# A four-layer transformer with a hybrid and an expert layer on one core: the first four mixers' projections and outputs as three rounded products

## The chip, the cores and the metric

The kernel runs on one core of one Trainium2 chip. The metric is the device time of one execution in microseconds (us), as the median over runs. A lower time is better.

## The reference

The input has 256 tokens (SEQ) and a width of 1024 (D). Four layers come first, each a feed-forward block, a mixer and a feed-forward block; a hybrid block and a mixture of experts follow and are no part of the change. What matters here:

```python
for i in range(DEPTH):                      # 4 layers
    x = x + 0.5 * rms_norm(swiglu(rms_norm(x, g[0]), ffn_w_in[i, 0], ffn_w_out[i, 0]), g[1])
    hm = rms_norm(x, g[2])
    if kind == 0:                           # layers 0 and 3: mixer A
        m = sliding_sink_attention(hm, a_w_in[j], a_w_out[j], a_sinks[j], rel_bias)
    elif kind == 1:                         # layer 1: mixer B
        m = nsa_attention(hm, b_w_in[j], b_w_out[j], ...)
    else:                                   # layer 2: mixer C
        m = moba_attention(hm, c_w_in[j], c_w_out[j], rel_bias)
    x = x + rms_norm(m, g[3])
    x = x + 0.5 * rms_norm(swiglu(rms_norm(x, g[4]), ffn_w_in[i, 1], ffn_w_out[i, 1]), g[5])
```

Every mixer is `h @ w_in` (queries of 16 heads of 64, keys, values; in B also six key and value sets and a gate), masked softmax attention with a relative bias, and `o @ w_out`. All inputs and the result are float32.

## The kernel before

Blocks run one after the other: ffn, A, ffn, ffn, B, ffn, ffn, C, ffn, ffn, A, ffn, then the hybrid and the experts. The residual x stays on chip. All weights come from HBM over SyncE's queue (`stream_weights`, L666) into a ring of three slots (`raw_ring`, RING is 3), one load of up to 512 columns or 512 rows in a slot; a slot is loaded again when its readers are done.

The feed-forward blocks (`pe_ffn`, L1289) don't use float32 products. A weight w is split: ScalarE copies it to the rounded type fp32r (w_hi, L1124 and L1131), VectorE subtracts that from the raw weight (w_lo, L1136 and L1143). h is split likewise. A product is then w_hi·h_hi + w_lo·h_hi + w_hi·h_lo, accumulated in PSUM. Lines L1298 and L1350 to L1352 are 512 columns wide (L1298 takes both halves of h beside each other), L1302 is 256.

The mixers use float32 products, which the hardware profile records as two matmuls each:

- `product` (L1411) computes an item: eight products over the eight 128-row parts of D. Form T (L1423) holds 128 columns of weights and moves h transposed (256 tokens): queries and keys. Form N (L1426) holds 128 tokens of h and moves up to 512 weight columns: values (128 wide in A, 256 in B, 512 in C), and B's gate of 48.
- `output` (L1497, product at L1499) multiplies the heads' result oT by the output weights, 512 columns at a time, in two halves c of four 128-row parts. The first half is `output_first`, four groups set between attention steps from `wo_step` on; the second is the mixer's last work on TensorE.

`mixer_layout` writes the order down by hand: the list of items, how many of them run ahead of the attention (`ahead`), and which run in step j (`steps`). A unit is one group of four heads and one half of 128 queries; step j does these on the engines:

- TensorE (L1404): scores of unit j (L1444), transposes of unit j−2 (L1463), the step's items, one `output_first`, values of unit j−2 (L1486 or L1491).
- VectorE (`dve_mixer`, L1555): the softmax coefficients of unit j−1 (L1616 to L1625), scale, bias and maximum of unit j (L1593 to L1608), copies of finished T items out of PSUM times the rows' scale (L1576, L1580), and the heads' result of unit j−2 copied to oT (L1635; added in B, L1633).
- ScalarE (`act_mixer`, L1657): the transposed probabilities of unit j−2 (L1692), the exponentials of unit j with their sums (L1677, in A also the sink, L1680), and N items out of PSUM (L1669).
- POOL (L1709): the probabilities times the coefficients (L1715).

Each engine runs its list in order, so an instruction that waits holds all that stands behind it. In the exponentials' loop VectorE's L1608 of unit j releases ScalarE's L1677, whose last one releases VectorE's L1616, behind which the scale and bias of unit j+1 stand. Item results lie in PSUM banks 2 and 3 in turn, scores in banks 0 and 1, transposes in 4 and 5, head results in 6 and 7.

Before a mixer's items, VectorE finishes the residual update (`dve_update`) and ScalarE makes h from the transposed x (L1014). Where a feed-forward block comes next, `dve_into_folded` (L984) sets the low halves of h (L978) between the parts of that update.

Of the kernel before, what the change touches and what calls it, by code (L numbers as in the profile page):

```python
# [149 lines left out]
class Attn:  # L150
# [11 lines left out]
    def vcol(self, quad, r, s):  # L162
        return {"A": quad // 2, "B": quad + 4 * s, "C": 4 * quad + r, "H": quad}[self.kind] * HD


class Semaphores:


    def __init__(self, nc, ctx):
        def some(names):  # L170
# [32 lines left out]
            some("proj evac_act evac_dve")  # L203

# [41 lines left out]
class Program:  # L246
# [19 lines left out]
    def map_memory(self):  # L266
# [23 lines left out]
        self.hT = new("hT", [P, KT, SEQ])  # L290
        self.gain_at = self.top
# [36 lines left out]
        b_start = self.cur  # L328
        self.zc = mix("cmp_tokens", [P, 2, G_B, SEQ])
# [130 lines left out]
    def plan(self):  # L460
        ins = self.ins
        fill = tile = item = unit = sunit = outs = 0
        split = used = folded = turned = mixers = posts = 0
        ev = {"act": 0, "dve": 0}
        self.fills = []
        for n, b in enumerate(self.blocks):
# [7 lines left out]
            if kind in ("ffn", "moe"):  # L474
                b["f"] = folded
                folded += 1
# [10 lines left out]
            else:  # L487
# [40 lines left out]
    def mixer_layout(self, b):  # L528
# [16 lines left out]
        def Q(f, r):  # L545
            T(f, 128 * (r % 4), self.qT[:, r, :])

        if kind == "A":
# [5 lines left out]
            N(kv, 128, 128, [self.v[:, a, 0:128] for a in range(NT)])  # L554
            for r in range(1, 8):
                Q(qs[r // 4], r)
            b["ahead"] = 6
            b["steps"] = [[6], [7], [8], [9], [10]]
            b["need_qk"] = [4, 6, 8, 10]
            b["need_v"] = [[2, 3]] * 4  # L560
            b["wo_step"] = 6
            wo = ins["a_w_out"][b["j"]]
        elif kind == "B":
# [20 lines left out]
            b["need_qk"] = [7, 9, 11, 13, 14, 14, 15, 15]  # L584
            b["need_v"] = [[4, 5]] * 4 + [[16, 17]] * 4
# [6 lines left out]
        elif kind == "C":  # L592
            w = ins["c_w_in"][0]
            vs, qs, ks = [], [], []
            vs.append(cols(w, (2 * D, 512)))
# [3 lines left out]
            vs.append(cols(w, (2 * D + 512, 512)))  # L599
# [4 lines left out]
            def V(c, a):  # L604
                items.append(dict(form="N", fill=vs[c], a=a, c0=0, n=512, dst=self.v[:, a, 512 * c:512 * c + 512]))

            Q(qs[0], 0), K(0), V(0, 0), V(0, 1), Q(qs[0], 1), K(1), Q(qs[0], 2)
            K(2), Q(qs[0], 3), K(3), Q(qs[1], 4), K(4), Q(qs[1], 5), K(5), V(1, 0)
            Q(qs[1], 6), K(6), Q(qs[1], 7), K(7), V(1, 1)
            b["ahead"] = 7  # L610
            b["steps"] = [[7, 8], [9, 10], [11, 12], [13, 14], [15, 16], [17, 18], [19]]
            b["need_qk"] = [5, 9, 13, 18]
            b["need_v"] = [[2, 3]] * 2 + [[14, 19]] * 2
            b["wo_step"] = 7
# [189 lines left out]

def x_order(b):
# [35 lines left out]
PRE_SS, PRE_V, PRE_R, POST_SS, POST_V, POST_R = 16, 20, 24, 32, 36, 40  # L841
# [133 lines left out]
def dve_low_h(K, dve, b, k):  # L975
# [3 lines left out]
    K.nc.vector.scalar_tensor_tensor(out=K.hT_lo[:, k, :], in0=turned_k(K, k), scalar=g,  # L979
                                     in1=K.hT_hi[:, k, :].bitcast(F32), op0=ALU.mult, op1=ALU.subtract)\  # L980
# [3 lines left out]
def dve_into_folded(K, dve, prev, b):  # L984
# [19 lines left out]
    dve_lo_dn(K, dve, 0, b["fill0"] % RING, b["tile0"] + 1)  # L1004


def act_into_turned(K, act, prev, b):
# [3 lines left out]
    def high(k):  # L1011
        g = K.gcol[:, f * KT + k:f * KT + k + 1]
        act.wait_ge(K.sem.x_tr, KT * f + k + 1)
        K.nc.scalar.activation(K.hT_hi[:, k, :] if folds(b) else K.hT[:, k, :], turned_k(K, k), ACT.Copy, scale=g)\  # L1014
            .then_inc(K.sem.hk_hi, 1)
# [13 lines left out]
    else:  # L1029
# [11 lines left out]
        high(7)  # L1041
    act.wait_ge(K.sem.r2_ps, f + 1)
# [104 lines left out]
def act_ffn(K, act, b):  # L1147
# [2042 lines left out]
```

## Time and profile before

| | before |
|---|---|
| median of 3 runs | 2689.94 us (2687.75, 2689.94, 2694.95) |
| profiled execution, span | 2692.0 us |
| TensorE matmuls, busy | 2642.6 us |
| TensorE weight loads, busy | 2087.1 us |
| VectorE | 1687.4 us |
| ScalarE | 1239.5 us |
| POOL | 239.1 us |
| mean granted TensorE clock | 0.988 |

The page reports one execution. A busy time counts each instruction from start to end; matmuls overlap their successors, so a rate is read from the starts of two groups in the timeline. "x16" is a number of instructions, and a float32 product is two of them. The granted clock is 1.00 at 2.4 GHz and 0.50 at 1.2 GHz.

### The profile page before, as it was taken

To read this page: it belongs to the slowest core of one execution; us is meant where nothing else is said; L and a number is where in the kernel's file an instruction comes from. 1 tells how busy PE (TensorE), PEld (TensorE's weight loads), DVE (VectorE), ACT (ScalarE), POOL (GpSimd) and SP (SyncE) were. 2 spreads that over 40 slices of the span, in tenths; PEclk is the share of its full clock that TensorE was granted. 3 is DMA by queue.
4 is the path that set the end of the run, shared out by engine and by line. 5 is a ranking of instruction groups with operands and counts; after the bars stand their busy time and mean duration, and the time that the engine had idled before them with its cause. 6 is when DMAs were issued, how large, how long until landed. Compare 5 with 4: busy or idle time off the path is not lost.

```text
span 2692.0 us, 36916 instructions
## 1 busy us (share of the span) xinstructions
PE 2642.6 (98%) x13112; PEld 2087.1 (78%) x13112; DVE 1687.4 (63%) x2560; ACT 1239.5 (46%) x1986; POOL 239.1 (9%) x364
## 2 busy tenths in 40 slices
PE   9999999999998999999999999999999999899999
PEld 7887688888874788888768888885888654688887
DVE  6764577777353777775237777745776552577776
ACT  5444544544333545544235455434543222366565
POOL 0001100100111100001010010012000001000000
PEclk9999999999997999999999999999999999999999
DMA  9542455554331555453255546433553322478885
GB/s 322 195 151 88 179 187 187 184 198 159 104 125 62 216 195 191 157 192 136 94 203 196 187 150 221 166 133 144 193 198 114 112 91 73 156 279 287 310 289 196
DMA packets 337244, 472.33 MB, mean 175 GB/s; under 512 B 15632, under 2 KB 275056, under 8 KB 337152
## 3 DMA queue, kind: packets, MB, share of 16 engines
q1 hardware_dynamic: 334464, 464.02, 48.1%
q0 software_dynamic: 2192, 6.94, 0.8%
q8 instruction: 54, 0.88, 0.1%
q14 instruction: 38, 0.31, 0.0%
q10 hardware_dynamic: 496, 0.17, 0.0%
HBM read 470.01 MB, written 1.10 MB: 175 GB/s over the span
## 4 chain that ended last, share of the span: by engine, by line
PE 92%; DVE 4%; ACT 2%; issue 1%; DMA 1%; POOL 0%; SPq 0%; DVEq 0%; ACTq 0%; POOLq 0%
PE psum_all L1298 22%; PE psum_all L1302 12%; PE psum_all L1423 6%; PE psum_all L1350 6%; PE psum_all L1351 6%; PE psum_all L1352 6%; PE psum_all L1499 4%; PE psum_all L1959 4%; PE psum_all L2919 3%; PE psum_all L2900 3%; PE psum_all L2896 3%; PE psum_all L2897 3%; PE psum_all L1426 2%; PE psum_all L2924 1%; PE psum_all L1444 1%; PE psum_all L1463 1%
## 5 line engine op out<-in xcount | busy, mean ns | idle before, releaser
L1298 PE MATMUL psum_all<-hT_both,gu_hi 128*128 128x512 f32 x2688 | 670.9, 391 | 0.3 <-DVE gu_lo L1136 0.3
L1298 PEld LDWEIGHTS psum_all<-hT_both,gu_hi 128*128 128x128 f32 x2688 | 492.8, 188 | 95.4 <-DVE gu_lo L1136 0.6
L1136 DVE TENSOR_TENSOR gu_lo<-raw_ring,gu_hi 128x2048 fp32r<-128x2048 f32 x176 | 402.0, 2286 | 14.1 <-ACT gu_hi L1124 9.6
L1302 PEld LDWEIGHTS psum_all<-hT_both,gu_lo 128*128 128x128 f32 x2688 | 366.7, 190 | 26.2
L1302 PE MATMUL psum_all<-hT_both,gu_lo 128*128 128x256 f32 x2688 | 374.8, 282 | 0.0
L1124 ACT ACTIVATE gu_hi<-raw_ring 128x2048 fp32r (+1 forms) x175 | 334.2, 1912 | 16.1 <-DVE oT L1635 12.2
L1131 ACT ACTIVATE down_hi<-raw_ring 128x1024 fp32r (+1 forms) x240 | 250.6, 1057 | 137.6 <-PE psum_all L1352 108.6
L1143 DVE TENSOR_TENSOR down_lo<-raw_ring,down_hi 128x1024 fp32r<-128x1024 f32 x240 | 292.4, 1218 | 34.1 <-ACT down_hi L1131 34.1
L1350 PE MATMUL psum_all<-down_hi,hidden_hi 128*128 128x512 f32 x704 | 277.2, 394 | 3.3 <-DVE hidden_lo L1230 2.6
L1351 PE MATMUL psum_all<-down_lo,hidden_hi 128*128 128x512 f32 x704 | 276.0, 392 | 0.0
L1352 PE MATMUL psum_all<-down_hi,hidden_lo 128*128 128x512 f32 x704 | 274.0, 389 | 0.0
L1278 POOL TENSOR_TENSOR hidden_hi<-hidden,consts_sb 128x256 fp32r<-128x256 f32 x176 | 108.1, 614 | 1293.4 <-DVE hidden L1226 1274.0
L1164 ACT ACTIVATE silu_gate<-silu_gate 128x256 f32<-128x256 f32 x176 | 73.5, 418 | 237.9 <-DVE silu_gate L1219 237.9
L1423 PE MATMUL psum_all<-hT,raw_ring 128*128 128x256 f32 x800 | 179.8, 380 | 0.0
L2750 DVE TENSOR_TENSOR e_gate_up_lo<-raw_ring,e_gate_up_hi 128x2048 fp32r<-128x2048 f32 x64 | 146.6, 2290 | 32.4 <-ACT e_gate_up_hi L2743 32.0
L1162 ACT ACTIVATE cross_terms<-psum_all 128x256 f32<-128x256 f32 x176 | 67.2, 382 | 214.0 <-PE psum_all L1302 214.0
L1423 PEld LDWEIGHTS psum_all<-hT,raw_ring 128*128 128x128 f32 x800 | 149.2, 190 | 21.1 <-issue 1.8
L1230 DVE TENSOR_TENSOR hidden_lo<-hidden,hidden_hi 128x256 fp32r<-128x256 f32 x176 | 74.8, 425 | 141.3 <-POOL hidden_hi L1278 141.3
L1350 PEld LDWEIGHTS psum_all<-down_hi,hidden_hi 128*128 128x128 f32 x704 | 132.8, 189 | 29.7 <-issue 5.2
L1352 PEld LDWEIGHTS psum_all<-down_hi,hidden_lo 128*128 128x128 f32 x704 | 132.2, 188 | 28.9
L1223 DVE TENSOR_TENSOR up_scaled<-psum_all,cross_terms 128x256 f32<-128x256 f32 x176 | 74.4, 423 | 127.5 <-ACT cross_terms L1166 127.5
L1351 PEld LDWEIGHTS psum_all<-down_lo,hidden_hi 128*128 128x128 f32 x704 | 132.9, 189 | 21.0
(379 smaller groups left out, 3519.4 us busy)
## 6 DMA issues: line engine op xcount, KB each, us to landing
raw_ring<-in_ffn_w_in SPq DMA_DIRECT2D x174, 1024.0 KB, 7.1
raw_ring<-in_w SPq DMA_DIRECT2D x96, 1024.0 KB, 7.8
raw_ring<-in_ffn_w_out SPq DMA_DIRECT2D x88, 1024.0 KB, 9.1
raw_ring<-in_c_w_in SPq DMA_DIRECT2D x12, 768.0 KB, 5.3
raw_ring<-in_w_in SPq DMA_DIRECT2D x10, 768.0 KB, 6.3
gain<-in_norm_g POOLq DMA_DIRECT2D x12, 512.0 KB, 4.0
raw_ring<-in_a_w_in SPq DMA_DIRECT2D x8, 768.0 KB, 5.3
raw_ring<-in_b_w_in SPq DMA_DIRECT2D x8, 768.0 KB, 5.0
```

What stands on the lines that cost most here:

```text
L1124: K.nc.scalar.activation(K.gu_hi[:, t, :, :], raw_gu(K, slot, t), ACT.Copy).then_inc(K.sem.gu_hi, 1)
L1131: K.nc.scalar.activation(K.dn_hi[:, t, :], raw_dn(K, slot, t), ACT.Copy).then_inc(K.sem.dn_hi, 1)
L1136: K.nc.vector.tensor_tensor(K.gu_lo[:, t, :, :], raw_gu(K, slot, t), K.gu_hi[:, t, :, :].bitcast(F32), ALU.subtract).then_inc(K.sem.gu_lo, 1)
L1143: K.nc.vector.tensor_tensor(K.dn_lo[:, t, :], raw_dn(K, slot, t), K.dn_hi[:, t, :].bitcast(F32), ALU.subtract).then_inc(K.sem.dn_lo, 1)
L1278: nc.gpsimd.tensor_tensor(K.hid_hi[:, t, :], K.hid[:, t, :], K.one.to_broadcast([P, SEQ]), ALU.mult)\
L1298: nc.tensor.matmul(out, K.gu_hi[:, t, j, :], K.hT_both[:, k, :, :].rearrange("p c s -> p (c s)"), start=k == 0, stop=False)
L1302: return nc.tensor.matmul(out[:, 0:SEQ], K.gu_lo[:, t, j, :], K.hT_hi[:, k, :], start=False, stop=k == KT - 1)
L1350: nc.tensor.matmul(out, h_hi, d_hi, start=first, stop=False)
L1351: nc.tensor.matmul(out, h_hi, d_lo, start=False, stop=False)
L1352: ins = nc.tensor.matmul(out, h_lo, d_hi, start=False, stop=last)
L1423: return nc.tensor.matmul(K.psum[:, bank, 0:SEQ], w[:, k, it["c0"]:it["c0"] + P], K.hT[:, k, :], start=k == 0, stop=k == KT - 1)
L2750: K.nc.vector.tensor_tensor(K.ge_lo[:, t, :, :, :].rearrange("p k g f -> p g k f"), raw_expert(K, b, n, t), K.ge_hi[:, t, :, :, :].rearran ...
```

## The change

In mixers A, B and C (four blocks: A twice) the projections and the output become three rounded products, as in the feed-forward blocks. `project` runs three parts for each 128-row part of D:

```python
    def product(q, k, part):
        turned, out, w, h = operands(q, k)
        wi, hi = ((0, 0), (1, 0), (0, 1))[part]
        lhsT, rhs = (w[wi], h[hi]) if turned else (h[hi], w[wi])
        return nc.tensor.matmul(out, lhsT, rhs, start=k == 0 and part == 0, stop=k == KT - 1 and part == 2)
```

Input weights are split in chunks of 256 columns (A 5, C 12, B 11, one of them 48 columns), output weights in four chunks of two 128-row parts (128x2048), all high halves on ScalarE and all low halves on VectorE, in place in the ring:

```diff
+def act_chunk_high(K, act, b, c):
+
+    x = b["chunks"][c]
+    raw, high, _, landed = chunk_views(K, b, c)
+    for j in range(3):
+        act.wait_ge(K.sem_raw[j], landed)
...
+    K.nc.scalar.activation(high, raw, ACT.Copy).then_inc(K.sem.mw_hi, 1)
...
+def dve_chunk_low(K, dve, b, c):
+
+    raw, high, low, _ = chunk_views(K, b, c)
+    dve.wait_ge(K.sem.mw_hi, b["chunk0"] + c + 1)
+    K.nc.vector.tensor_tensor(low, raw, high.bitcast(F32), ALU.subtract).then_inc(K.sem.mw_lo, 1)
...
+def act_rows_high(K, act, b, c):
...
+    K.nc.scalar.activation(high, raw, ACT.Copy).then_inc(K.sem.wo_hi, 1)
...
+def dve_rows_low(K, dve, b, c):
...
+    dve.wait_ge(K.sem.wo_hi, 4 * b["mix"] + c + 1)
+    K.nc.vector.tensor_tensor(low, raw, high.bitcast(F32), ALU.subtract).then_inc(K.sem.wo_lo, 1)
```

Two chunks of each mixer are split at the end of the feed-forward block before it, the third beside h; chunk c's high half stands three items ahead of its first user in ScalarE's list, the low half two items ahead in VectorE's. The output weights' splits have steps of their own (`wo_act`, `wo_dve`), here those of A:

```diff
+            b["wo_act"] = {2: [0], 3: [1], 5: [2], 6: [3]}
+            b["wo_dve"] = {3: [0], 4: [1], 6: [2], 7: [3]}
```

B has {13, 14, 16, 17} and {14, 15, 17, 18}, C has 5, 6 and twice 8, and 6, 7 and twice 9.

h's low half is made by `dve_into_folded`, which now also serves these mixers. Queries are no longer multiplied by the rows' scale on VectorE; ScalarE copies them (L1899), and the scale is a part of the scores' scale (Q_SCALE). The heads' result is split too. In A and C both halves are made from PSUM:

```diff
     def copy_out(x):
         dve.wait_ge(K.sem.oPV, U0 + x["u"] + 1)
-        dst = K.oT[:, 2 * x["quad"]:2 * x["quad"] + 2, x["a"] * P:(x["a"] + 1) * P]
         src = K.psum[:, 6 + x["u"] % 2, 0:2 * P].rearrange("p (t s) -> p t s", t=2)
+        if kind != "B":
+            dve.wait_ge(K.sem.oT_high, 8 * b["mix"] + x["u"] + 1)
+            nc.vector.tensor_tensor(quad_of(K.oT_lo[kind], x), src, quad_of(K.oT_hi[kind], x).bitcast(F32),
+                                    ALU.subtract).then_inc(K.sem.oT_sb, 1)
+            return
...
+    def out_high(x):
+        u, a = x["u"], x["a"]
...
+            act.wait_ge(K.sem.oPV, U0 + u + 1)
+            src = K.psum[:, 6 + u % 2, 0:2 * P].rearrange("p (t s) -> p t s", t=2)
+        nc.scalar.activation(dst, src, ACT.Copy).then_inc(K.sem.oT_high, 1)
...
+        for c in b["wo_act"].get(j, ()):
+            act_rows_high(K, act, b, c)
+        if kind != "B" and j >= 2 or j >= 18:
+            out_high(units[j - 2])
```

In B the heads' result is gathered in oT as before; from step 18 on ScalarE makes the high halves and VectorE the low ones (L1852). Orders of items change: in C the values are four pieces of 256 columns instead of two of 512, the list is Q0 K0 Q1 K1 V0 Q2 Q3 K2 K3 V1 Q4 Q5 Q6 Q7 K4 K5 V2 K6 K7 V3 (each V two items) with `ahead` 8 and

```diff
-            b["ahead"] = 7
-            b["steps"] = [[7, 8], [9, 10], [11, 12], [13, 14], [15, 16], [17, 18], [19]]
...
+            b["ahead"] = 8
+            b["steps"] = [[8, 9, 10], [11, 12], [13, 14, 15], [16, 17, 18], [19, 20], [21, 22], [23]]
```

In B the second key item and Q1 stand earlier. A keeps its order. SyncE's loads keep their order and POOL its instructions.

ScalarE in the first mixer A, step 2 and the start of step 3, before (L1677 are the exponentials, L1692 the transposed probabilities):

```order
L1677 ACTIVATE scores_first,attn_den<-scores_first,attn_max 128x128 x4
L1680 ACTIVATE attn_sink_exp<-attn_sink_exp 128x4
L1692 ACTIVATE probsT<-psum_all 128x1024
L1677 ACTIVATE scores,attn_den<-scores,attn_max 128x256 x4
L1680 ACTIVATE attn_sink_exp<-attn_sink_exp 128x4
```

and in the change:

```order
L1910 ACTIVATE scores_first,attn_den<-scores_first,attn_max 128x128 x4
L1913 ACTIVATE attn_sink_exp<-attn_sink_exp 128x4
L1899 ACTIVATE qT<-psum_all 128x256
L962 ACTIVATE raw_high<-raw_ring 128x2048
L1937 ACTIVATE oT_hi<-psum_all 128x2x128
L1925 ACTIVATE probsT<-psum_all 128x1024
L1910 ACTIVATE scores,attn_den<-scores,attn_max 128x256 x4
```

Between a unit's exponentials and the next unit's there stand now a query copy, an output weight split and the high half of the heads two units back.

VectorE at the same place, maximum of unit 2 to the scale and bias of unit 3, before (L1616 to L1625 are unit 2's coefficients):

```order
L1608 TENSOR_SCALAR attn_max<-attn_max 128x4
L1580 TENSOR_TENSOR qT<-psum_all,rstd_rows 128x256
L1635 COPY oT<-psum_all 128x2x128
L1616 TENSOR_TENSOR attn_den<-attn_den,attn_sink_exp 128x4
L1617 TENSOR_SCALAR attn_den<-attn_den 128x4
L1625 RECIPROCAL attn_coef<-attn_den 128x4
```

and in the change:

```order
L1812 TENSOR_SCALAR attn_max<-attn_max 128x4
L1839 TENSOR_TENSOR oT_lo<-psum_all,oT_hi 128x2x128
L1820 TENSOR_TENSOR attn_den<-attn_den,attn_sink_exp 128x4
L1821 TENSOR_SCALAR attn_den<-attn_den 128x4
L1829 RECIPROCAL attn_coef<-attn_den 128x4
L1797 SCALAR_TENSOR_TENSOR scores<-psum_all,stats,bias_window 128x4x128
```

The query product has gone from VectorE, and in the place of the plain copy stands a subtraction that reads ScalarE's L1937.

VectorE near the end of mixer B in the change, from the last scale of the compressed probabilities on:

```order
L2056 TENSOR_TENSOR cmp_probs<-cmp_probs,cmp_stats 128x240
L969 TENSOR_TENSOR raw_low<-raw_ring,w_hi_spare 128x2048
L1845 TENSOR_TENSOR oT<-psum_all,oT 128x2x128
L1821 TENSOR_SCALAR attn_den<-attn_den 128x4
L1825 RECIPROCAL attn_den<-attn_den 128x4
L1826 TENSOR_TENSOR attn_coef<-attn_den,b_gate 128x4
L1845 TENSOR_TENSOR oT<-psum_all,oT 128x2x128
L969 TENSOR_TENSOR raw_low<-raw_ring,raw_high 128x2048
L1845 TENSOR_TENSOR oT<-psum_all,oT 128x2x128
```

The two L969 are new there; the other rows stood in the same order before.

## Rows read from the trace of the kernel before

**Rows 1.** The page, part 1: busy us, share of the span, instructions of each engine

```profile
PE 2642.6 (98%) x13112; PEld 2087.1 (78%) x13112; DVE 1687.4 (63%) x2560; ACT 1239.5 (46%) x1986; POOL 239.1 (9%) x364
```

**Rows 2.** The page, part 4: the chain that ended last, by engine

```profile
PE 92%; DVE 4%; ACT 2%; issue 1%; DMA 1%; POOL 0%; SPq 0%; DVEq 0%; ACTq 0%; POOLq 0%
```

**Rows 3.** The page, part 5: costliest groups (busy us, mean ns, idle before)

```profile
L1136 DVE TENSOR_TENSOR gu_lo<-raw_ring,gu_hi 128x2048 fp32r<-128x2048 f32 x176 | 402.0, 2286 | 14.1 <-ACT gu_hi L1124 9.6
...
L1124 ACT ACTIVATE gu_hi<-raw_ring 128x2048 fp32r (+1 forms) x175 | 334.2, 1912 | 16.1 <-DVE oT L1635 12.2
...
L1423 PEld LDWEIGHTS psum_all<-hT,raw_ring 128*128 128x128 f32 x800 | 149.2, 190 | 21.1 <-issue 1.8
```

**Rows 4.** Timeline of TensorE, float32 products (start us, us; two records a product)

```profile
230.07 2.05 PE L1426 MATMUL psum_all<-raw_ring,hT 128*128 128x128 f32 x16 [0.91 <-DVE qT L1580]
...
291.86 14.00 PE L1499 MATMUL psum_all<-raw_ring,oT 128*128 128x512 f32 x32 [0.54 <-DVE oT L1635]
...
697.13 1.88 PE L1426 MATMUL psum_all<-raw_ring,hT 128*128 128x48 f32 x16
...
720.92 0.71 PE L1444 MATMUL psum_all<-kT,qT 64*128 64x128 f32 x8
...
1276.99 13.90 PE L1426 MATMUL psum_all<-raw_ring,hT 128*128 128x512 f32 x32
1290.73 10.52 PE L1423 MATMUL psum_all<-hT,raw_ring 128*128 128x256 f32 x48
1301.18 0.71 PE L1444 MATMUL psum_all<-kT,qT 64*128 64x128 f32 x8
```

**Rows 5.** Timeline of TensorE in a feed-forward block, rounded products

```profile
963.65 1.98 PE L1298 MATMUL psum_all<-hT_both,gu_hi 128*128 128x512 f32 x8
965.47 1.11 PE L1302 MATMUL psum_all<-hT_both,gu_lo 128*128 128x256 f32 x8
966.42 1.32 PE L1298 MATMUL psum_all<-hT_both,gu_hi 128*128 128x512 f32 x5
```

**Rows 6.** Timeline of VectorE and ScalarE in the first mixer A: the softmax loop

```profile
252.62 0.17 DVE L1608 TENSOR_SCALAR attn_max<-attn_max 128x4 f32<-128x4 f32 x1
...
269.23 0.17 DVE L1608 TENSOR_SCALAR attn_max<-attn_max 128x4 f32<-128x4 f32 x1
...
271.42 0.19 ACT L1680 ACTIVATE attn_sink_exp<-attn_sink_exp 128x4 f32<-128x4 f32 x1
...
271.64 0.16 DVE L1616 TENSOR_TENSOR attn_den<-attn_den,attn_sink_exp 128x4 f32<-128x4 f32 x1 [1.72 <-ACT attn_sink_exp L1680]
...
274.45 0.17 DVE L1608 TENSOR_SCALAR attn_max<-attn_max 128x4 f32<-128x4 f32 x1
...
279.88 0.17 DVE L1608 TENSOR_SCALAR attn_max<-attn_max 128x4 f32<-128x4 f32 x1
```

**Rows 7.** Timeline of the first mixer A: copies of 256 columns from PSUM

```profile
227.42 0.38 ACT L1043 ACTIVATE rstd_rows<-psum_all 128x256 f32<-128x256 f32 x1 [2.92 <-PE psum_all L1090]
...
269.50 0.42 DVE L1635 COPY oT<-psum_all 128x256 f32<-128x256 f32 x1
```

**Rows 8.** Stretches of mixers A and C: busy us (count) by engine, PEclk, DMA, GB/s

```profile
256.00:270.00 14.00, 12.89 (x86) 9.32 (x84) 10.38 (x27) 6.56 (x24) 3.23 (x3) 1.00 0.31 100
...
1310.00:1380.00 70.00, 70.00 (x368) 49.87 (x367) 24.81 (x51) 20.08 (x65) 11.57 (x8) 1.00 0.45 165
```

**Rows 9.** Stretches near the end of mixer B: PE, PEld, DVE, ACT, POOL, PEclk

```profile
815.00:820.00 5.00, 4.76 (x76) 4.39 (x76) 3.49 (x10) 2.56 (x9) 1.17 (x1) 1.00 0.39 156
820.00:830.00 10.00, 7.24 (x38) 4.21 (x36) 9.38 (x26) 5.51 (x20) 1.76 (x2) 0.57 0.00 1
830.00:840.00 10.00, 5.43 (x23) 2.99 (x24) 2.89 (x12) 1.44 (x2) 1.89 (x1) 0.50 0.00 0
```

**Rows 10.** Timeline of TensorE, first outputs of mixer B

```profile
851.38 5.66 PE L1499 MATMUL psum_all<-raw_ring,oT 128*128 128x512 f32 x8
...
857.99 3.60 PE L1499 MATMUL psum_all<-raw_ring,oT 128*128 128x512 f32 x8
```

More of the change, by code:

```diff
@@ L491, in plan @@
                 b["loads"], b["items"] = self.mixer_layout(b)
+                if splits(b):
+                    b["f"] = folded
+                    folded += 1
+                    b["chunk0"], b["mix"] = chunk, split_mixers
+                    chunk += len(b["chunks"])
+                    split_mixers += 1
                 for q, it in enumerate(b["items"]):
-                    it["by"] = "dve" if it["form"] == "T" else "act"
+                    it["by"] = "dve" if it["form"] == "T" and not it.get("query") else "act"
                     ev[it["by"]] += 1
@@ L545, in Q, with chunk @@
         def Q(f, r):
-            T(f, 128 * (r % 4), self.qT[:, r, :])
+            T(f, 128 * (r % 4), self.qT[:, r, :], query=True)
+        b["chunks"] = []
+        def chunk(f, c0, place, n=SEQ):
+            mine = [q for q, it in enumerate(items) if it["fill"] == f and c0 <= it["c0"] < c0 + n]
+            b["chunks"].append(dict(fill=f, c0=c0, n=n, place=place, first=mine[0], last=mine[-1]))
+            for q in mine:
+                items[q]["chunk"] = len(b["chunks"]) - 1
         if kind == "A":
@@ new lines, in dve_chunk_low @@
+def dve_chunk_low(K, dve, b, c):
[3 more added lines that the diff above has]
+def act_rows_high(K, act, b, c):
+    raw, high, _, landed = rows_views(K, b, c)
+    for j in range(3):
+        act.wait_ge(K.sem_raw[j], landed)
+    last = len(b["items"]) if b["kind"] != "A" or c == 3 else 0
+    if b["wo_place"][c] != "tail" and last:
+        act.wait_ge(K.sem.proj, b["item0"] + last)
+    if b["kind"] == "B" and c == 3:
+        act.wait_ge(K.sem.z2, 2)
+    K.nc.scalar.activation(high, raw, ACT.Copy).then_inc(K.sem.wo_hi, 1)
@@ L1041, in act_into_turned @@
         high(7)
+        if splits(b):
+            act_chunk_high(K, act, b, 2)
     act.wait_ge(K.sem.r2_ps, f + 1)
@@ L1431, in project @@
             wait_evac(K, pe, b, q - 2)
+        wait_chunk(items[q]["chunk"])
         for k in range(KT):
-            ins = product(q, k)
+            for part in range(3):
+                ins = product(q, k, part)
         ins.then_inc(K.sem.proj, 1)
@@ L1518, in pe_mixer @@
     pe_turn_x(K, pe, b, 0)
+    wait_chunk(items[0]["chunk"])
+    wait_chunk(items[1]["chunk"])
     for k in range(KT):
         if k == 3:
-            pe.wait_ge(K.sem.hk_hi, KT * turn + k + 1)
             pe_turn_x(K, pe, b, 1)
         pe.wait_ge(K.sem.hk_hi, KT * turn + k + 1)
-        for q in range(2):
-            ins = product(q, k)
-            if k == KT - 1:
-                ins.then_inc(K.sem.proj, 1)
+        for part in range(3):
+            if part == 2:
+                pe.wait_ge(K.sem.hk_lo, KT * b["f"] + k + 1)
+            for q in range(2):
+                ins = product(q, k, part)
+                if k == KT - 1 and part == 2:
+                    ins.then_inc(K.sem.proj, 1)
     pe_rstd_rows(K, pe, b)
@@ L1562, in evacuate_turned @@
         it, bank = items[q], item_bank(q)
-        if it["form"] != "T":
+        for c, x in enumerate(b["chunks"]):
+            if c > 2 and max(x["first"] - 2, 0) == q:
+                dve_chunk_low(K, dve, b, c)
+        if it["by"] != "dve":
             return
```

264 lines of the change are left out of this document (204 added, 60 removed).

## The prediction

> **What bounds the kernel now.** The page's first part comes first: TensorE is busy 98% of the 2692.0 us, VectorE 63%, ScalarE 46% [rows 1]; the chain of waits runs over TensorE for 92% [rows 2]. So TensorE time counts, unless the change makes it wait. Next the costliest groups: a split of 2048 columns takes ScalarE 1.91 us and VectorE 2.29 us, and the mixers' L1423 product has 800 weight loads of 0.190 us [rows 3], two for each product, so 400 products. The timeline then gives rates by start-to-start times, because the durations of overlapping matmuls count time twice. Last I read the mixers' own stretches, where ScalarE and VectorE are no bystanders: in a step of mixer A one loop runs VectorE (scale, bias, maximum) to ScalarE (exponentials) and back to VectorE (coefficients), and that loop, not TensorE, is nearly its length already.
>
> **TensorE, per product.** fp32, 256 columns: 48 records (24 products) from 1290.73 to 1301.18, 0.435 us each [rows 4]. A rounded product of 256 columns: eight from 965.47 to 966.42, 0.119; of 512 columns eight from 963.65 to 965.47, 0.228 [rows 5]. Three of 0.119 are 0.357: 0.078 less for each of 400, −31.2. The output's 512-column product: 32 records in 13.8, 0.864 each [rows 4], now 3 × 0.228 = 0.684: −0.18 for each of 128, −23.0. C's values were 32 products of 512 columns, 32 records (16 products) in 13.74, 0.859 each [rows 4], now 64 of 0.357: −4.7. B's values, 32 products: −2.5. Against it, products of 128 columns (A's values, 32) and of 48 columns (B's gate, 16) now cost about 0.236 each: 16 records, eight products, take 2.05 and 1.88, some 0.1 of it overlap with the next [rows 4]. No rounded product under 256 columns is in the trace. Lower end: 3 × 0.119 × 128/256 = 0.18, a gain; upper end: each as slow as the whole fp32 product, 3 × 0.236 = 0.71. I take 0.357, nearest to the measured rounded product, because a weight load of 0.190 [rows 3] stands before each, wide or narrow: 48 × 0.12 = +5.8. Net −55.6 of TensorE work. The first two items of each mixer (64 products, −5.0) follow the low halves of h that VectorE now makes behind the residual update, so I let that gain go: about −51 would be the ideal.
>
> Here a rule speaks. The rows say that three rounded products cost 82% of an fp32 product at 256 columns, 79% at 512. The Trainium skill ("FP8 and Floating Point Precision", TensorE Precision Notes) says true FP32 is 4 passes through the array; three of four would be 75%. By that rule the products concerned, 337 us (400 and 32 at 0.435, 128 at 0.864, 32 at 0.859, 48 at 0.236), would lose a quarter, 84 us, an estimate from that page; by rows 4 and 5 it is 51. The sum goes by the rows.
>
> **Mixer A, twice: a longer loop.** The old loop from one maximum to the next (L1608) took 5.22 and 5.43 us [rows 6], mean 5.33: maxima, exponentials until 271.42 + 0.19, coefficients at 271.64, next maxima at 274.45. The old head copy L1635 (0.42 [rows 7]) lay inside it for nothing, while ScalarE worked. In the change the low half of the heads (L1839) stands at the end of VectorE's step, waits for ScalarE's high half (L1937), and the next step's coefficients are queued behind it; and L1937 stands at the end of ScalarE's step, behind the exponentials, the copy of a projection and the 2048-column split of an output weight (L962). So each step that has heads is now in series: ScalarE's copy 0.38 and VectorE's 0.42 [rows 7] and two handovers (one such takes 0.03, from 271.61 on ScalarE to 271.64 on VectorE [rows 6]; I allow 0.15 for both), 0.95 in all; +0.38 where a projection copy stands before it (three of the five intervals); +1.91 where a weight split stands before it (steps 2, 3, 5, 6, four intervals) [rows 3]. Five intervals, from the maximum of 252.62 to that of 279.88, were 27.3 [rows 6]; now 5 × (5.33 + 0.95) + 3 × 0.38 + 4 × 1.91 = 40.2, +12.9. TensorE, busy 12.9 of 14 in 256 to 270 [rows 8], will idle 2 to 3 of some 8 us in each step, so its gains there don't count. VectorE's own split of 2.29 lies beside the exponentials and copies of its step and costs nothing. After the last maximum: the four first outputs have then been done (−0.4), and the second half, 16 products of 0.864, gets 2.9 shorter. **A: +9.6 each, +19.2.**
>
> **Mixer C.** TensorE is busy 70.0 of 70 us in 1310 to 1380 [rows 8]: its step is longer than the loop. Eight items of its head instead of seven come before the first scores: two values items and four others (48 products) for the old 24.2 us from 1276.99 to 1301.18 [rows 4], 17.1 now: −7.1. The remaining projections −6.3, outputs −5.8. But steps 5, 6 and 8 hold L962 (two of them in step 8), and the last steps have few projections, so the same serial piece stalls TensorE in steps 5 to 8. A step of TensorE there is some 3.5 of scores, transposes and values and 2.86 (8 × 0.357) for each item: step 5 with two items is 9.2 and covers the loop's 5.33 + 0.95 + 1.91 = 8.2; step 6 with one item is 6.4 and stalls 1.8; step 7 with none stalls 6.3 − 3.5 = 2.8; in step 8 two splits (3.8) stand before the copy that the last values wait for, 3.0 of them bare. 7.6 come back. **C: −11.6.**
>
> **Mixer B.** Its heads are copied as before, and the high and low halves come only from step 18 on. Its head from 697.13 to the first scores at 720.92 [rows 4], 23.8 us, becomes seven items of 2.86 = 20.0 and starts 0.2 later: −3.6. The compression comes 9.2 earlier: 13 more items give 8.1, less what VectorE's token sums before it hold back. But in 820 to 830 VectorE is busy 9.38 of 10 us and TensorE waits for it [rows 9]: in that chain stand two output weight splits (4.6), the low halves (0.5) and scale reads (0.8). Outputs −6.1, last pair of halves +0.9. **B: −9.2 + 4.6 + 0.5 + 0.8 − 6.1 + 0.9 = −8.5.**
>
> **The clock.** After 815 to 820 with narrow matmuls the granted clock falls to 0.57 and 0.50, half of 2.4 GHz, while TensorE is busy 5 to 7 of 10 us [rows 9], and eight output records take 5.66 instead of 3.60 [rows 10]. A's steps will be busy some 70%. Lower bound nothing, upper bound half clock through A's last steps (below). I take half of that row's 2.06 for each of three mixers, +3.0. Off the path: loads (SP's order is the same, slots come free no later than now), POOL (same instructions), the query copies moved from VectorE to ScalarE (0.38 each, priced above where they stand in the loop).
>
> Sum: 19.2 − 11.6 − 8.5 + 3.0 = **+2.1**. The profiled execution's span was 2692.0; the median of the runs, 2689.94, is 2.1 below. So 2694.1 in a profile, **2692** as a median.
>
> **Rivals.**
> (1) *The serial piece is hidden, TensorE paces* (0.20). It would need heads' halves to be ready before the exponentials end; the order of both queues speaks against it, TensorE's 98% for it. If half is hidden, A costs +5 less each and C 5 less: about 2677. Fully hidden: 2690 − 51 = 2639, chance 0.05 of the 0.20.
> (2) *Rounded products at three quarters of fp32, and nothing waits*: 0.326 us for three of 256 columns, 84 us less, 2606; rows 5 show 0.357 and 0.684 and speak against it. Chance 0.01. It is what the page's rule would give.
> (3) *Slower: half clock in A* (0.30). Mechanism: TensorE's idle pieces between 256 and 304 make the granted clock fall, as in rows 9. At half clock its work of a step (some 6 us with an output, at full) becomes 12, more than the 8 of the loop, and the second outputs begin at half clock. It decides from the point where the clock stays at 0.5 for two steps in a row. Price: 2 steps × 3 + 2 per A, 16 for both, and 3 in C: 2692 + 19 − 3 = 2708. Narrow products at 0.71 instead of 0.357 would add another 17 (0.35 × 48); I give that 1 in 10.
> (4) *Forecast case* (0.49): own range 2681 to 2703.
>
> **Range and chances.** 2664 to 2714 leaves out the fully hidden case and the sum of half clock and narrow products. A measurement tells about 0.3%, 8 us, from no change. Faster than 2682: (1), (2) and an eighth of (4), 0.27. Slower than 2698: (3) nearly whole and a seventh of (4), 0.36. Same: 0.37.
>
> **What would show it.** Right: in A maxima 8 to 8.7 us apart in steps with L962 and some 6.5 without; L1839 waiting on L1937, and L1820 right behind it; TensorE idle over 10 us between 256 and 304 against 2 before; the stretch of A 9 to 10 us longer, that of C some 12 and of B 8 to 9 shorter; the items' rounded products at 0.119 start to start. Wrong: TensorE idle in A under 5 us (rival 1); granted clock 0.5 in A's steps (rival 3); narrow products far from 0.357.

## The result and the profile after

| | before | after |
|---|---|---|
| median of 20 runs each, same chip | 2694.2 us (2684.48 to 2698.64) | 2700.69 us (2694.67 to 2706.67) |
| ratio | | 1.0028, 95% interval 1.0018 to 1.0039 |
| profiled execution, span | 2692.0 us | 2699.6 us |

All ratios are of fast executions; a single slow one, 2886.82 us at a granted clock of 0.84, in e11 below, is left out of its ratio.

The change costs 0.3%, though TensorE is busy 33 us less. The page of the changed kernel, part 1, and the engines of its chain (part 4):

```profile
PE 2609.3 (97%) x13848; PEld 2135.9 (79%) x13848; DVE 1798.4 (67%) x2621; ACT 1345.8 (50%) x2103; POOL 242.0 (9%) x364
...
PE 83%; DVE 9%; ACT 5%; issue 2%; DMA 1%; POOL 0%; SPq 0%; DVEq 0%; ACTq 0%; POOLq 0%
```

Against [rows 1, 2] TensorE's matmuls fell from 2642.6 to 2609.3 us, VectorE rose by 111 and ScalarE by 106. TensorE's share of the chain fell by 9 points; 8 of them went to VectorE and ScalarE. Where this happens is read from landmarks of both timelines: a mixer's first projection product, and the first matmul behind its last output.

| us | before | after | difference |
|---|---|---|---|
| start to first A | 218.99 | 221.22 | +2.2 |
| first A | 86.70 | 93.64 | +6.9 |
| to B | 383.21 | 384.44 | +1.2 |
| B | 196.74 | 193.58 | −3.2 |
| to C | 383.12 | 383.97 | +0.9 |
| C | 133.83 | 128.96 | −4.9 |
| to second A | 383.16 | 383.90 | +0.7 |
| second A | 86.71 | 93.64 | +6.9 |
| to the end | 819.5 | 816.2 | −3.3 |

With the stretch ahead of each, where its first weights are split, the As cost 9.2 and 7.7, B gives 1.9 and C 4.0. The last row has the same code in both kernels. In the traces of the experiments below it lasts 816 to 821 us whatever the mixers do, so its 3.3 is no effect of the change.

The loop of the first A on VectorE, unit 2's maximum to unit 3's, as in [rows 6]:

```profile
253.71 0.17 DVE L1812 TENSOR_SCALAR attn_max<-attn_max 128x4 f32<-128x4 f32 x1
...
258.11 0.42 DVE L1839 TENSOR_TENSOR oT_lo<-psum_all,oT_hi 128x256 fp32r<-128x256 f32 x1 [4.22 <-ACT oT_hi L1937]
258.45 0.15 DVE L1820 TENSOR_TENSOR attn_den<-attn_den,attn_sink_exp 128x4 f32<-128x4 f32 x1
...
262.00 0.17 DVE L1812 TENSOR_SCALAR attn_max<-attn_max 128x4 f32<-128x4 f32 x1
```

and ScalarE at the same time:

```profile
255.48 0.19 ACT L1913 ACTIVATE attn_sink_exp<-attn_sink_exp 128x4 f32<-128x4 f32 x1
...
255.84 1.90 ACT L962 ACTIVATE raw_high<-raw_ring 128x2048 fp32r<-128x2048 f32 x1
257.64 0.37 ACT L1937 ACTIVATE oT_hi<-psum_all 128x256 fp32r<-128x256 f32 x1
```

The exponentials end at 255.67. The coefficients that need only them start at 258.45, because L1839 stands ahead of them and waits 4.22 us for L1937, which stands behind L962. The maxima come at 253.71, 262.00, 269.95, 276.44, 284.13 and 292.16: 38.45 us for five intervals, 27.3 before.

TensorE meanwhile, in stretches of 10 us (busy us and count of PE, PEld, DVE, ACT, POOL, then PEclk, DMA share, GB/s):

```profile
255.00:265.00 10.00, 8.03 (x68) 6.94 (x66) 6.05 (x11) 6.71 (x20) 1.04 (x1) 1.00 0.01 2
265.00:275.00 10.00, 6.57 (x28) 3.83 (x28) 7.65 (x17) 5.50 (x15) 2.94 (x2) 0.59 0.88 315
275.00:285.00 10.00, 5.92 (x24) 4.31 (x21) 5.31 (x14) 5.39 (x15) 1.90 (x1) 0.67 0.00 1
285.00:295.00 10.00, 10.00 (x54) 6.86 (x53) 7.64 (x13) 6.82 (x21) 1.04 (x1) 0.89 0.01 2
295.00:305.00 10.00, 8.47 (x46) 5.90 (x45) 1.61 (x6) 3.30 (x5) 1.90 (x1) 1.00 0.19 59
```

It idles 11.0 us in these 50. In the same 50 us of the kernel before it idled 1.6, and the granted clock was 1.00 throughout; now it reads 0.59 in one stretch. The loop hides even that: the interval 269.95 to 276.44, most of it at half clock, is 6.5 us, what the loop alone asks for (5.33 + 0.95 + 0.38 = 6.7).

TensorE's waits in C from its first scores on (us in total, times, longest):

```profile
PE psum_all L1611 <- ACT v_tok L1902: 2.8, 1, 2.8
PE psum_all L1689 <- DVE raw_low L969: 2.7, 1, 2.7
PE psum_all L1678 <- ACT probsT L1925: 2.2, 1, 2.2
PE psum_all L1611 <- ACT qT L1899: 2.0, 1, 2.0
```

In [rows 8] TensorE was busy 70.0 of 70 us there. The first and last of these waits (before 1322.76 and 1330.78) go back to ScalarE and VectorE, ten to twenty us earlier:

```profile
1311.28 1.91 ACT L942 ACTIVATE raw_high<-raw_ring 128x2048 fp32r<-128x2048 f32 x1 [3.93 <-DMA raw_ring<-in_c_w_in]
...
1318.47 0.51 ACT L1910 ACTIVATE scores<-scores,attn_max 128x256 f32<-128x256 f32 x1 [4.91 <-DVE attn_max L1812]
```

```profile
1313.22 2.29 DVE L949 TENSOR_TENSOR raw_low<-raw_ring,raw_high 128x2048 fp32r<-128x2048 f32 x1 [4.09 <-ACT raw_high L942]
1315.43 0.16 DVE L1821 TENSOR_SCALAR attn_den<-attn_den 128x4 f32<-128x4 f32 x1
```

A weight split set three items ahead meets a load that has not landed. ScalarE waits for it, VectorE waits for ScalarE, and the coefficients, the next maximum and ScalarE's copy of V stand behind both. The other two waits come at 1374.11 and 1378.95, among the output weights' splits.

The granted clock falls in C too, twice (PE busy and count, PEclk, DMA share, GB/s); in the kernel before it read 1.00 from C's first product to its end:

```profile
1331.00:1336.00 5.00, 5.00 (x34) 0.66 0.00 0
1379.00:1384.00 5.00, 5.00 (x20) 0.66 0.01 5
```

In B, the two output weight splits in VectorE's chain, as expected, and a third beside POOL:

```profile
831.10 2.28 DVE L969 TENSOR_TENSOR raw_low<-raw_ring,raw_high 128x2048 fp32r<-128x2048 f32 x1
...
840.59 2.29 DVE L969 TENSOR_TENSOR raw_low<-raw_ring,w_hi_spare 128x2048 fp32r<-128x2048 f32 x1
...
843.96 3.86 DVE L969 TENSOR_TENSOR raw_low<-raw_ring,raw_high 128x2048 fp32r<-128x2048 f32 x1
```

and TensorE around B's 48 narrow gate products, which start from 712.8 to 718.6 (PE busy and count, PEclk, DMA share, GB/s; stretches of 5 us, the first from 10 us after B's first product):

```profile
709.31:714.31 5.00, 5.00 (x46) 1.00 0.30 35
714.31:719.31 5.00, 5.00 (x38) 0.80 0.00 0
719.31:724.31 5.00, 5.00 (x26) 0.52 0.00 0
724.31:729.31 5.00, 5.00 (x44) 1.00 0.19 32
```

The kernel before has a milder fall at the same place, behind its 32 records of the gate (697.1 to 701.7):

```profile
702.00:707.00 5.00, 5.00 (x16) 0.67 0.00 0
```

### The profile page after: what moved, and what is told of

Same layout as the page of the kernel before. It is cut to its first block, busy times and chain, and to the rows that moved or that the text cites. A ratio compares the mean times of both kernels' runs of the same rounds, so it can differ in the third digit from the quotient of the medians.

```text
span 2699.6 us, 38653 instructions
## 1 busy us (share of the span) xinstructions
PE 2609.3 (97%) x13848; PEld 2135.9 (79%) x13848; DVE 1798.4 (67%) x2621; ACT 1345.8 (50%) x2103; POOL 242.0 (9%) x364
## 4 chain that ended last, share of the span: by engine, by line
PE 83%; DVE 9%; ACT 5%; issue 2%; DMA 1%; POOL 0%; SPq 0%; DVEq 0%; ACTq 0%; POOLq 0%
PE psum_all L1477 22%; PE psum_all L1481 11%; PE psum_all L1529 6%; PE psum_all L1530 6%; PE psum_all L1531 5%; PE psum_all L1611 4%; PE psum_all L2207 4%; PE psum_all L3148 3%; PE psum_all L3167 3%; PE psum_all L3144 2%; PE psum_all L3145 2%; PE psum_all L3172 1%; PE psum_all L2329 1%; PE psum_all L2348 1%; DVE attn_max L1807 1%
## 5 line engine op out<-in xcount | busy, mean ns | idle before, releaser
L1333 ACT ACTIVATE cross_terms<-psum_all 128x256 f32<-128x256 f32 x176 | 67.2, 382 | 207.2 <-PE psum_all L1481 207.2
L1396 DVE TENSOR_TENSOR silu_gate<-silu_gate,rstd_rows 128x256 f32<-128x256 f32 x176 | 75.0, 426 | 87.0 <-ACT silu_gate L1335 87.0
L1337 ACT ACTIVATE cross_terms<-psum_all 128x256 f32<-128x256 f32 x176 | 66.9, 380 | 128.4 <-PE psum_all L1481 128.4
```

## The experiments

Theory: in A the serial piece (exponentials, split, L1937, L1839, coefficients) sets the pace, not TensorE. Rival: TensorE's own time, at half clock, sets it. Ratios are to the kernel before, run on the same chip in the same rounds; the change has 1.0028.

**e1: the heads' high half ahead of the weight split.**

```diff
-        for c in b["wo_act"].get(j, ()):
-            act_rows_high(K, act, b, c)
         if kind != "B" and j >= 2 or j >= 18:
             out_high(units[j - 2])
+        for c in b["wo_act"].get(j, ()):
+            act_rows_high(K, act, b, c)
```

> In mixers A and C ScalarE's high half of the heads (L1937) stands ahead of the output weight's split (L962) instead of behind it; nothing else moves. Serial theory (the loop maximum - exponentials - L1937 - L1839 - coefficients sets A's pace): the four steps of A with a split get 1.9 us shorter each, maxima some 6.4 apart instead of 8.0 to 8.3, A -7.6 each, C -1 to -2: about 2684 against the change's 2700.7, ratio to before 0.996 to 0.998. Rival (TensorE, at half clock from 267 on, sets the pace): within 3 us of the change, ratio 1.002 to 1.004.

Measured 2685.88 us, ratio 0.9968 (0.9956 to 0.9979), in the range of the serial theory. The first A's maxima from 253.64 on are 6.5, 6.2, 6.5, 5.9 and 6.7 apart; A lasts 87.8 us instead of 93.64. The total expected, 2684, is met within 2 us. The move of one 1.9 us instruction past one of 0.4 gives back 0.6%.

**e2: both halves of the heads one step later,** on VectorE at the end of the step, on ScalarE ahead of the exponentials. Two pieces of the edit; A's `wo_step` goes from 6 to 7 besides, with two output groups in its last step:

```diff
-        if j >= 2:
+        if kind != "B" and 3 <= j <= len(units):
+            copy_out(units[j - 3])
+        if j >= (2 if kind == "B" else len(units)):
             copy_out(units[j - 2])
...
             copy_pT(units[j - 2])
+        if kind != "B" and 3 <= j <= len(units):
+            out_high(units[j - 3])
         if j < len(units) and units[j]["si"] is not None:
             exps(units[j])
```

> In A and C both halves of a unit's heads are made one step later: ScalarE's before the step's exponentials, VectorE's after the step's maximum, so that no coefficient is queued behind a wait for ScalarE; A's first outputs start a step later, two of them in its last step. Serial theory: A's maxima 5.3 to 5.6 apart again, A -11 each, C -3, total -25: about 2676, ratio 0.993 to 0.995, and TensorE's granted clock in A stays at 1.00. Rival (TensorE's own time or its half clock sets the pace): at most -5, ratio 1.001 or more.

Measured 2683.78 us, ratio 0.9963 (0.9949 to 0.9976). VectorE in the first A:

```profile
263.04 0.17 DVE L1812 TENSOR_SCALAR attn_max<-attn_max 128x4 f32<-128x4 f32 x1
265.32 0.42 DVE L1839 TENSOR_TENSOR oT_lo<-psum_all,oT_hi 128x256 fp32r<-128x256 f32 x1
269.22 0.17 DVE L1812 TENSOR_SCALAR attn_max<-attn_max 128x4 f32<-128x4 f32 x1
269.30 0.42 DVE L1839 TENSOR_TENSOR oT_lo<-psum_all,oT_hi 128x256 fp32r<-128x256 f32 x1
274.43 0.17 DVE L1812 TENSOR_SCALAR attn_max<-attn_max 128x4 f32<-128x4 f32 x1
```

L1839 waits for nothing any more and the maxima are 5.2 to 6.2 apart, as before the change. A lasts 87.1 us, C 123.7. The gain is 17 us and not 25: A is back where it was (86.7), not below. Its outputs now start later, at 278.61; e10 tests whether that is the cause. The granted clock was expected to stay at 1.00 and did not; it reads 0.90 in 265 to 275 and 0.76 in 275 to 285.

**e3: float32 outputs, rounded projections.** `output` and `copy_out` as before the change, no L962, L969, L1937.

> The output products of all four mixers are float32 again (no splits of output weights, no halves of the heads; one copy by VectorE as before the change); the projections stay three rounded products. Serial theory: A loses the loop's extra (-11) and gets its second half of outputs 2.9 longer: -8 each; B -6 of chain, +6 of outputs, 0; C -3 + 6 = +3: about 2687, ratio 0.997. If TensorE's time counts in full instead, the 23 us of outputs come back: 2724, ratio 1.011.

Measured 2683.11 us, ratio 0.9959 (0.9945 to 0.9974). Giving back 23 us of TensorE's gain makes the kernel 0.7%, some 18 us, faster than the change. A lasts 86.2 and 85.3 us, B 191.7. C lasts 127.5, no longer than in the change, where 3 us more were expected (e2's C, with rounded outputs, is 3.8 shorter).

**e4: B's first two output weight splits earlier.**

```diff
-            b["wo_act"] = {13: [0], 14: [1], 16: [2], 17: [3]}
-            b["wo_dve"] = {14: [0], 15: [1], 17: [2], 18: [3]}
+            b["wo_act"] = {10: [0, 1], 16: [2], 17: [3]}
+            b["wo_dve"] = {10: [0], 11: [1], 17: [2], 18: [3]}
```

> In mixer B the first two splits of output weights go from steps 13 to 15 to steps 10 and 11, where VectorE waits for TensorE's compression. Theory that these two L969 (2.28 and 2.29 us) lie bare in VectorE's chain at 831 and 840: B -4.6, about 2696, ratio 1.0011. Rival (the chain's end is set by TensorE at half clock, or they only move the wait): within 1 us of the change.

Measured 2694.27 us, ratio 1.0001 (0.9992 to 1.0009). B lasts 188.0 us instead of 193.6. The profiled B also has a milder clock fall at its start: first scores 29.0 after its first product, 30.6 in the change. That is no effect of the edit, since e2 and e6, whose B is that of the change, show 29.0 too, and e1 32.2. It accounts for 1.6 of the 5.6; 4.0 are the splits, 4.6 were expected.

**e5: two items a step in C.**

```diff
-            b["steps"] = [[8, 9, 10], [11, 12], [13, 14, 15], [16, 17, 18], [19, 20], [21, 22], [23]]
+            b["steps"] = [[8, 9], [10, 11], [12, 13, 14], [15, 16, 17], [18, 19], [20, 21], [22], [23]]
```

> Mixer C alone: two items a step instead of three in step 0, and so on by one item later. The trace of the change shows VectorE held 4.1 us (L949 behind ScalarE's L942, which waits 3.9 us for a load) ahead of the coefficients, and TensorE idle 2.8 and 2.0 us a step later. Theory (split queued ahead of the softmax of the same step): those stalls go, C -4 to -5, about 2696, ratio 1.001. Rival (TensorE's work in C sets its length, the stalls come back elsewhere): within 1.5 us of the change, ratio 1.002 to 1.003.

Measured 2694.98 us, ratio 1.0013 (1.0000 to 1.0027). C lasts 122.2 us in the profile against 128.96 in the change and 126.2 to 127.9 in e4, e6 and e9, whose C is that of the change. TensorE's waits of 2.8 and 2.0 us are gone; two at the end, 3.3 and 1.6, remain. So 4 to 6 us, as the theory has it; the interval of the total alone would not part it from the rival.

**e6: the first A's second split ahead of the bias copies.**

```diff
+    if splits(after):
+        act_chunk_high(K, act, after, 1)
     if n == 0 and K.uses_bias:
         act_bias(K, act)
...
-    if splits(after):
-        act_chunk_high(K, act, after, 1)
```

> Ahead of the first mixer A ScalarE makes the second chunk's high half before the eight bias copies instead of after them, so VectorE's L949 no longer holds the residual update. Theory: A's first product comes 1.3 to 1.6 us earlier (221.22 in the change, some 219.8 here), the total by as much, about 2699, less than a measurement can tell; the look at the trace decides. Rival: the residual update is held by the other split, no change of that start.

Measured 2698.83 us, ratio 1.0021 (1.0009 to 1.0033): not told apart from the change. The profiles say more. In the four that have the edit (e6, e7, e10, e11) A's first product comes at 218.15 to 219.31, in the seven of the change and its other variants at 219.61 to 221.22. The two groups don't overlap, and their means are 1.8 us apart; 1.3 to 1.6 were expected.

**e7: e2, e4, e5 and e6 together.**

> Later halves of the heads in A and C (as e2), B's first two output weight splits at steps 10 and 11 (as e4), C's steps (as e5) and the earlier split before the first A (as e6), together. If the pieces lie in different mixers and so add up: 2700.7 - 17 - 6.5 - 4 - 1.5 = about 2672, ratio 0.9915 to 0.993. If they share one wait, less than 20 in all: above 2680.

Measured 2675.73 us, ratio 0.9929 (0.9916 to 0.9941). The single gains, as differences of ratios, sum to 0.0114; together they give 0.0099. They nearly add up. C, which e2 and e5 both shorten, is where some may be shared: 123.7 and 122.2 us alone, 120.3 together.

**e8: the serial piece alone, in the kernel before.** The kernel before, with two copies at the end of ScalarE's step in A and a wait ahead of VectorE's copy of the heads. TensorE's outputs wait for the added copies too. Pieces of the edit:

```diff
+        if b["kind"] == "A":
+            pe.wait_ge(K.sem.wo_hi, 4 * b["j"] + 2 * (c + 1))
...
+        if kind == "A":
+            dve.wait_ge(K.sem.oT_high, 8 * b["j"] + x["u"] + 1)
...
+            if j in (2, 3, 5, 6):
...
+                nc.scalar.activation(K.loop_rows[:, :], K.raw[:, slot, c % 2 * 2 * D:(c % 2 + 1) * 2 * D],
+                                     ACT.Copy).then_inc(K.sem.wo_hi, 1)
+            if j >= 2:
...
+                nc.scalar.activation(K.loop_heads[:, :, :],
+                                     K.psum[:, 6 + u % 2, 0:2 * P].rearrange("p (t s) -> p t s", t=2),
+                                     ACT.Copy).then_inc(K.sem.oT_high, 1)
```

> The kernel before (all mixer products float32, TensorE's work untouched), to which mixer A alone gets the change's serial pieces: after the exponentials ScalarE copies 128x2048 of an output weight to a scratch place in steps 2, 3, 5 and 6 and the unit's heads to another, and VectorE's copy of the heads waits for the latter. The result doesn't use either copy. Serial theory: five intervals of 0.95 more and four of 1.91 more, +12.4 for each A, at least +10: about 2694 + 23 = 2717, ratio 1.008 to 1.010. Rival (TensorE with 98% busy covers it): under +5 in all, ratio under 1.002.

Measured 2713.72 us, ratio 1.0070 (1.0058 to 1.0083). VectorE's maxima in the first A:

```profile
252.26 0.17 DVE L1614 TENSOR_SCALAR attn_max<-attn_max 128x4 f32<-128x4 f32 x1
...
260.15 0.17 DVE L1614 TENSOR_SCALAR attn_max<-attn_max 128x4 f32<-128x4 f32 x1
...
289.88 0.17 DVE L1614 TENSOR_SCALAR attn_max<-attn_max 128x4 f32<-128x4 f32 x1
```

Five intervals take 37.6 us, 38.45 in the change, 27.3 before. The As last 97.5 and 98.9 us, 10.8 and 12.2 more. TensorE's work is untouched here, and its longest wait, 4.3 us ahead of the first outputs, is for VectorE's copy of the heads and not for the added weight copies. So this is the price of the serial piece by itself; 98% busy did not cover it. In the change some of it is paid back: the head of A is 1.0 us shorter and the stretch behind the last maximum, with the last outputs, 3.1.

**e9: B's gate with one product instead of three.**

```diff
-            for part in range(3):
+            for part in range(1 if items[q].get("gate") else 3):
                 ins = product(q, k, part)
```

> In mixer B the gate's 16 products of 48 columns are one rounded product each (w_hi times h_hi) instead of three; the small terms of the gate are left out. Own time of 32 narrow matmuls: -3.6. In the trace of the change the granted clock reads 0.86 and 0.80 in the 20 us after them. Theory (the narrow ones bring the clock down, the more the longer they run): the first scores of B come 5 to 7 us earlier after its first product (24 us instead of 29 to 30.6) and the clock in those stretches reads 0.95 or more. Rival (clock has another cause): 3.6 earlier only, the clock as before. Total 2694 to 2697, ratio 1.000 to 1.0015.

Measured 2693.28 us, ratio 0.9996 (0.9983 to 1.0010). First scores 24.5 us after B's first product. TensorE in the stretches that follow the gate:

```profile
713.00:718.00 5.00, 4.61 (x40) 1.00 0.00 0
718.00:723.00 5.00, 5.00 (x44) 1.00 0.16 28
```

The clock stays at 1.00, as the theory asked. Of the 6.1 us by which B's head is shorter than in the change, 3.6 are the 32 matmuls themselves (0.112 each, below); the other 2.5 are what is left for the clock. Against the profiles with the milder fall (29.0) that rest is 0.9.

**e10: e7, with A's unit 3 halved early and C's last splits spread.** In A `out_high` and `copy_out` of unit 3 go to step 5 and `wo_step` is 6 again; C's `wo_act` is 5, 6, 7, 8.

> As e7, but in A unit 3's heads are halved already in step 5 (ScalarE ahead of that step's exponentials, where it waits 2.7 us in e7), so that the first output group runs in step 6, in TensorE's idle 4.9 us ahead of values(4), and one group a step follows; in C the last two output weight splits go from step 8 (9) to steps 7 and 8 (8 and 9). Theory: A ends 2.7 earlier, each (one group's 2.73 us leaves the tail), C 1 to 3 earlier (its stall of 3.0 ahead of the last values): about 2675.7 - 7 = 2669, ratio 0.990 to 0.992. Rival (the tail of A waits for POOL and ScalarE, not for TensorE): at most -2, ratio 0.993.

Measured 2671.57 us, ratio 0.9920 (0.9903 to 0.9936). The first A lasts 82.9 us, 4.0 less than in e7 and 3.8 less than before the change, so the late outputs did hold e2 back. The theory had 2.7; the granted clock also stayed at 1.00 through both As here, which may be the rest. C lasts 120.35 (e7: 120.33), with the same 3.0 us stall: there the expectation missed. By the totals alone e10 is not told apart from e7 (their intervals overlap); the two profiled As show the gain. This is the lowest median, 0.8% below the kernel before and 1.1% below the change.

**e11: B's gate products interleaved with its values' products.**

> e10 with B's gate products (three rounded ones each, nothing left out) interleaved one by one with its values' products of 256 columns instead of standing in one block of 48; same matmuls, other order. Theory (a long run of narrow matmuls brings the clock down, as e9 showed): the granted clock stays at 0.95 or more in the 20 us after, B's first scores come 26 to 27.5 us after its first product instead of 29.0, total -2 to -3.5 against e10: about 2669, ratio 0.990 to 0.992. Rival (their number counts, not their run): first scores at 29 as in e10, ratio 0.992.

Measured 2678.16 us, ratio 0.9946 (0.9927 to 0.9964): a miss. The first scores of B come 37.9 us after its first product. TensorE from 700 on:

```profile
700.00:705.00 5.00, 4.01 (x36) 1.00 0.00 0
705.00:710.00 5.00, 2.56 (x19) 0.85 0.00 0
710.00:715.00 5.00, 5.00 (x25) 0.50 0.00 0
715.00:720.00 5.00, 5.00 (x24) 0.50 0.00 0
```

The new order made it wait 1.4 us for a split and 2.4 for a copy in the midst of the narrow products, and the clock halved for over 10 us. The order was not the only thing that changed. So whether a run of narrow products alone, or their number, brings the clock down stays open.

## Why the prediction was right, and where its steps were off

**The total.** Forecast was +2.1 us for a profiled execution, as the sum 19.2 − 11.6 − 8.5 + 3.0; measured is +7.6, as 16.9 − 4.0 − 1.9 − 3.3 (the As, C, B, the unchanged end). By medians 2692 was forecast and 2700.69 came; the kernel before, measured beside it, took 2694.2 where 2689.94 had been shown. It lies inside the range and inside the likeliest case's own. The thought behind it, that A's longer loop eats what B and C gain, was right. That the total came so near is in part luck: B and C gained 14 us less than written, and 9 of them were made up by A, by the end and by the allowance for the clock, for reasons that have nothing to do with B and C. Of the signs that were named, L1839's wait and TensorE's idle time in A came as written, and the maxima nearly (7.7 to 8.3 apart for 8 to 8.7). The lengths did not: A 6.9 longer for 9 to 10, C 4.9 shorter for 12, B 3.2 shorter for 8 to 9.

**TensorE, per product: right.** Three rounded products of 256 columns take 0.360 us (0.12 apart, the last three rows), 0.357 was priced. The narrow ones, whose bounds were 0.18 and 0.71, were priced 0.357 and take 3 × 0.112 (the first three):

```profile
229.52 0.28 PE L1611 MATMUL psum_all<-raw_high,mT_lo 128*128 128x128 f32 x1
229.63 0.28 PE L1611 MATMUL psum_all<-raw_high,mT_hi 128*128 128x128 f32 x1
229.74 0.28 PE L1611 MATMUL psum_all<-raw_low,mT_hi 128*128 128x128 f32 x1
...
234.61 0.28 PE L1611 MATMUL psum_all<-mT_lo,raw_high 128*128 128x256 f32 x1
234.73 0.28 PE L1611 MATMUL psum_all<-mT_hi,raw_high 128*128 128x256 f32 x1
234.85 0.28 PE L1611 MATMUL psum_all<-mT_hi,raw_low 128*128 128x256 f32 x1
```

So three rounded products of 128 columns (0.336) are dearer than one float32 product (0.236), as forecast. The reason shows in the starts of the kernel before: its float32 records of 48 and 128 columns follow one another after 0.112 us too (median), those of 256 columns after 0.216, where a rounded one needs 0.12. Narrow products gain nothing by rounding, and there are three of them for two records.

**Mixer A: the mechanism right.** The loop was to grow by 12.9, it grew by 11.2 (38.45 for 40.2). The As were to cost 9.6 each. With the stretch ahead they cost 9.2 and 7.7, but A itself only 6.9: the loop's 11.2, less 1.1 ahead of it, which the forecast had at nothing, less 3.1 behind it for 3.3. The rest, 2.2 and 0.7, lies ahead of A's first product, where the forecast had nothing either. e1, e2 and e8 show the mechanism by taking it away in two ways and by adding it to the kernel before.

**Mixer C: the sum failed at the stalls and at the clock.** Forecast −11.6, measured −4.0. The head's −7.1 came as −7.3. "7.6 come back" was laid out for steps 5 to 8 only; the waits there came to 4.9. The input weights' own splits were put at nothing, and they cost another 4.8 us of TensorE's waits in the first steps, behind a load, L942 and L949. e5, which moves one item a step, takes just these away and gives 4 to 6 us back. The forecast had 1.0 for the clock in each mixer; two stretches of 5 us at 0.66 (above) are up to 3.4 us, an estimate from these rows. With 9.7 of waits and 3.4 of clock the sum gives some −6, measured is −4.9 in C itself and 0.9 more ahead of it. In e4, e6 and e9, with the same code in C, it is −6.0 to −7.7.

**Mixer B: the mechanism right, the sum missed.** Forecast −8.5, measured −1.9. The two bare splits were priced 4.6; e4 gives 4.0. The head gave 1.4 for 3.6; in the profiles with the milder clock fall, which the kernel before has too, it gave 3.0. So most of what is missing there is the longer fall of this one profile. Another 1.4 is missing up to the compression (waits of 1.1 for V and of 2.8 for 1.4), 1.8 near the end, where VectorE's split beside POOL took 1.6 longer, and 1.2 ahead of B's first product.

**The clock in A (+3.0 allowed, rival 3): half right.** It fell, to 0.59 and 0.67, as rival 3 said, but cost nothing that can be seen, since the loop was longer still. Where it cost was B and, by the estimate above, C.

**Rival 1 (TensorE paces, gains count)** is refuted for A by e8: of the 12.4 us expected for each A, 10.8 and 12.2 came out in its length, for all the 98% busy on the page.

**The rule on passes.** Three rounded products cost 83% of one float32 product at 256 columns (0.360 of 0.435) and 79% at 512, measured in the changed mixers. By the Trainium skill ("FP8 and Floating Point Precision", TensorE Precision Notes) it would be three of four passes, 75%; the measurement decides.

## What to carry to other kernels

Busy share does not say what an instruction costs on a side engine: look for the loop between engines, compare its length with TensorE's step, and ask of every instruction added to a queue whether something of that loop stands behind it. A product that is handed from ScalarE to VectorE should be consumed a step later than it is made; here that one rule, without any change of the work, turned +0.3% into −0.4%, and with the splits moved to idle places and A's outputs early again −0.8%. Split weights when their load has landed and the engine waits anyway, not a fixed number of items ahead. One profile shows one execution: the same code in B's head took 29.0, 30.6 and 32.2 us, so a difference of a us or two in a stretch wants several profiles.

## What the runs showed of the hardware

- A rounded matmul of 48 or 128 columns follows the one before after 0.112 us, one of 256 columns after 0.12, one of 512 after 0.227 (medians of the change): half the columns, 128 for 256, save 7%. A float32 record takes 0.112 at 48 and 128 columns, 0.216 at 256 and 0.429 at 512 (kernel before).
- TensorE can be recorded busy 5.00 of 5 us and still be granted 0.52 of its clock, behind 48 matmuls of 48 columns; with 16 of them (e9) the clock stayed at 1.00. With the same code the fall is milder in some profiles (0.87 and 0.79 in e6).
- A subtraction of 2048 columns on VectorE took 3.86 instead of 2.29 us while POOL ran a 1024-column multiplication (843.78 to 845.67). The ten profiles whose B has this split show it at the same place, 3.86 each time. In the change no other split of 2048 columns runs beside so long an instruction of POOL's. In the change L1812 (4 columns) also took 0.58 to 0.60 us the ten times that POOL multiplied beside it, and ended within 0.03 us of POOL each time; the other 30 times it took 0.17. The split ended 2.15 us behind POOL's end, nearly its own 2.29. So VectorE looks held until POOL was done rather than slowed; no run tests it by itself.
